# Row spacing of the split weights in a two-layer decoder step, and where the rotary tables lie

## The reference, cut to what matters

```
xp = xp + rmsnorm(mixer(rmsnorm(xp, g_mix_pre)), g_mix_post)      # layer 0: attention + short convolution
xp = xp + rmsnorm(ffn(rmsnorm(xp, g_ffn_pre)), g_ffn_post)        # layer 1: gated spatial MLP as the mixer
def ffn(h, w_up, w_down):
    a = jax.nn.relu(h @ w_up)                                     # 2048 -> 8192
    return (a * a) @ w_down                                       # 8192 -> 2048
def rope(x, pos):                                                 # on queries and keys of layer 0
    return jnp.concatenate([x1 * cos - x2 * sin, x2 * cos + x1 * sin], axis=-1)
```

## Time and profile before

| | us |
|---|---|
| median of 3 runs | 2230.07 |
| lowest and highest of them | 2228.09, 2232.19 |
| the profiled execution | 2228.98 |
| its span, first to last instruction | 2227.3 |
| PE busy in the span | 2176.4 |
| PEld busy | 2154.9 |
| DVE busy | 1249.9 |
| ACT busy | 995.6 |
| POOL busy | 236.9 |

### The profile page before, as it was taken

The page is one execution under the profiler, slowest core; times in us unless marked ns, Lnnn a source line. Parts: engine busy times, 40 slices in busy tenths (PEclk is TensorE's granted clock), DMA queues, the critical chain, the costliest instruction groups (busy, mean ns, idle before and its releaser), DMA issues.

```text
span 2227.3 us, 43497 instructions
## 1 busy us (share of the span) xinstructions
PE 2176.4 (98%) x17771; PEld 2154.9 (97%) x17771; DVE 1249.9 (56%) x1318; ACT 995.6 (45%) x1243; POOL 236.9 (11%) x178
## 2 busy tenths in 40 slices
PE   7999998999999999999989999989999999999999
PEld 7999998999999999999979999979999999999998
DVE  7556756654554455455576675575445545545543
ACT  5545444443443344344454564444334434434443
POOL 3001213000000000011251201220000000001112
PEclk9999998999999999999999999989999999999999
DMA  6854453655655655565535455545555555555551
GB/s 218 232 171 136 155 183 113 189 177 181 187 174 186 215 181 186 176 185 172 186 114 188 155 170 181 178 127 176 188 175 183 183 177 187 174 184 183 176 181 65
DMA packets 380630, 386.72 MB, mean 174 GB/s; under 512 B 6804, under 2 KB 378316, under 8 KB 380430
## 3 DMA queue, kind: packets, MB, share of 16 engines
q1 hardware_dynamic: 374530, 380.02, 54.4%
q10 hardware_dynamic: 6036, 5.80, 0.8%
HBM read 380.10 MB, written 5.71 MB: 173 GB/s over the span
## 4 chain that ended last, share of the span: by engine, by line
PE 92%; DVE 6%; ACT 1%; DMA 0%; issue 0%; DVEq 0%; SPq 0%; ACTq 0%
PE ps L1353 30%; PE ps L1355 30%; PE ps L1354 30%; DVE hlo L979 2%; DVE wlo L952 1%; DVE y L1001 1%; ACT whi L586 0%; PE ps L1635 0%; DMA region<-in_x_prompt_dram 0%; PE ps L1704 0%; PE ps L1548 0%; PE ps L1534 0%; PE ps L1467 0%; DVE region L1336 0%; DVE y L1006 0%; DVE x L1007 0%
## 5 line engine op out<-in xcount | busy, mean ns | idle before, releaser
L952 DVE TENSOR_TENSOR wlo<-raw,whi 128x1024 fp32r<-128x1024 f32 x712 | 895.2, 1261 | 805.0 <-ACT whi L586 804.6
L586 ACT ACTIVATE whi<-raw 128x1024 fp32r<-128x1024 f32 x712 | 752.3, 1059 | 1066.4 <-PE ps L1355 1061.3
L1353 PE MATMUL ps<-hhi,whi 128*128 128x264 f32 x3136 | 902.6, 288 | 33.4 <-DVE hlo L979 33.1
L1354 PE MATMUL ps<-hlo,whi 128*128 128x264 f32 x3136 | 895.4, 286 | 0.0
L1355 PE MATMUL ps<-hhi,wlo 128*128 128x264 f32 x3136 | 895.3, 285 | 0.0
L1353 PE MATMUL ps<-ahi,whi 128*128 128x264 f32 x2560 | 727.0, 284 | 0.0
L1355 PE MATMUL ps<-ahi,wlo 128*128 128x264 f32 x2560 | 726.8, 284 | 0.0
L1354 PE MATMUL ps<-alo,whi 128*128 128x264 f32 x2560 | 726.6, 284 | 0.0
L1353 PEld LDWEIGHTS ps<-hhi,whi 128*128 128x128 f32 x3136 | 595.5, 190 | 43.5 <-issue 30.1
L1355 PEld LDWEIGHTS ps<-hhi,wlo 128*128 128x128 f32 x3136 | 595.4, 190 | 0.0
L1354 PEld LDWEIGHTS ps<-hlo,whi 128*128 128x128 f32 x3136 | 595.1, 190 | 0.1
(11 more groups left out here) (218 smaller groups left out, 763.6 us busy)
## 6 DMA issues: line engine op xcount, KB each, us to landing
raw<-in_w_ffn_up_dram SPq DMA_DIRECT2D x128, 1024.0 KB, 5.3
raw<-in_w_ffn_down_dram SPq DMA_DIRECT2D x128, 1024.0 KB, 5.5
raw<-in_w_in_even_dram SPq DMA_DIRECT2D x36, 1024.0 KB, 5.1
raw<-in_w_in_cmlp_dram SPq DMA_DIRECT2D x32, 1024.0 KB, 5.3
raw<-in_w_out_even_dram SPq DMA_DIRECT2D x16, 1024.0 KB, 5.5
raw<-in_w_out_cmlp_dram SPq DMA_DIRECT2D x16, 1024.0 KB, 5.6
region<-in_x_prompt_dram SPq DMA_DIRECT2D x4, 512.0 KB, 9.1
out_y_prompt_dram<-region SPq DMA_DIRECT2D x8, 256.0 KB
```

Of the source, the lines that this page charges most:

```text
L586: act.activation(whi[:, QK * q:QK * q + QK, :], raw[:, 2 * par + q // 2, k, :], ACT.Copy).then_inc(w_hi_ready, 1)
L952: dve.tensor_tensor(wlo[:, QK * q:QK * q + QK, :], raw[:, 2 * par + q // 2, k, :], whi[:, QK * q:QK * q + QK, :].bitcast(F32), ALU.subtrac ...
L1353: pe.matmul(out, whi[:, k, cols], hi[:, k, ::-1], start=(k == 0), stop=False)
L1354: pe.matmul(out, whi[:, k, cols], lo[:, k, ::-1], start=False, stop=False)
```

## The change

The tiles whi and wlo get rows of 264 words, of which the first 256 are used. A row therefore takes 1056 bytes, as a row of the activations does. This needs 512 bytes more for each of the two tiles. The tiles cos and sin are no longer allocated; their names now stand for rows 14 and 15 of y. The compiled addresses are now: whi 33920, wlo 50816, hhi 101504, hlo 118400, ahi 135296, alo 152192. Every engine has the same instructions in the same order as before, with the same waits; the write of whi and the write of wlo now go to four pieces of 256 words, 264 apart, where they went to 1024 words in one piece. Tiles declared after sin lie 1088 bytes lower than before, those from x to mean_w 1024 bytes higher.

```diff
@@ -52,6 +52,7 @@
 BC = 256
+WROW = T
@@ -93,8 +94,8 @@
         raw = sb("raw", [P, 4, 2 * QK, BC])
-        whi = sb("whi", [P, CH, BC], F32R)
-        wlo = sb("wlo", [P, CH, BC], F32R)
+        whi = sb("whi", [P, CH, WROW], F32R)[:, :, 0:BC]
+        wlo = sb("wlo", [P, CH, WROW], F32R)[:, :, 0:BC]
@@ -104,8 +105,8 @@
-        cos = sb("cos", [P, T])
-        sin = sb("sin", [P, T])
+        cos = y[:, 14, :]
+        sin = y[:, 15, :]
```

## The result

| | before | changed |
|---|---|---|
| median, first comparison | 2230.07 (5 runs) | 2219.06 (5 runs, 2216.87 to 2221.27) |
| median, second comparison (after_again) | 2230.08 (9 runs) | 2218.65 (5 runs, 2217.33 to 2219.21) |
| profiled execution, and its span | 2228.98, 2227.3 | 2220.41, 2218.7 |

The ratio is 0.9951 with an interval of 0.9937 to 0.9966 in the first comparison and 0.9948 (0.9934 to 0.9961) in the second: faster by 11.0 and by 11.4 us. The forecast was 2218.1, with a range of 2212.0 to 2229.5.

A forecast was written before the change was run, and what follows sets the result against it. PE's matmul pace was taken as the bound, slowed where its two reads meet. 172 blocks times 0.07 us gave 12.0 us, other parts nothing: 2228.98 to 2216.98, plus 1.09 for the median, 2218.1; range 2212 to 2229.5.

The forecast's parts named there:

- Reading of the bound: PE's matmul pace sets the time; rows 2, 3 and 4 of eight together take 2.20 us instead of 2.16.
- phases 64 to 128: Distance from weight row to activation row, modulo 256 bytes; at these values PE's two reads were said to meet.
- The slower weight load of the earlier trace: Over k = 2 and 3 PE's weight load is listed with 189 ns instead of 188, cited as showing both streams matter.
- Saving per block: Sixteen clean rows make a block of 11.52 to 11.55 us instead of 11.60: 0.05 to 0.08 us saved, 0.07 taken.
- Number of blocks: 172 blocks gain, without block 0, the first after each of three normalisations and two more around the layer-1 mixer.
- The inner band: Total of 2213 to 2222 us around 2218.1, from savings of 13.9 and 8.3 with 1 us of scatter; chance 0.72.
- Writes in four pieces: Writes of whi and wlo by ACT and DVE: costed at nothing, between -20 and +20 ns a write.
- loads from any multiple of 32 bytes: PE weight loads now start at any multiple of 32 bytes, as the transposes' loads already do: nothing.
- the tables: cos and sin in rows 14 and 15 of y: same shapes, no wait added, nothing.
- the constant phase be a bad one: Rival: the one distance now paid in every row is slow, 11.76 us a block, 2257.6 us in all; chance 0.07.

The follow-up runs named there:

- after_again: The changed kernel unaltered, run again against the kernel before: 2218.65 us, ratio 0.9948.
- before_shift128: The kernel before with a gap of 32 unused words ahead of x, moving the activations under the old weight spacing: 2228.99 us.
- half_load: The changed kernel computing only 64 of 128 columns in the low by high and high by low products (but for row 15 of high by low): 2216.80 us.
- phase32: The changed kernel with a gap of 8 unused words ahead of x, distance 32 bytes modulo 256 in every row: 2219.26 us.
- phase192: The changed kernel with a gap of 48 unused words ahead of x, distance 192 bytes modulo 256 in every row: 2217.13 us.
- tables_alone: The kernel before with only cos and sin moved into rows 14 and 15 of y: 2229.98 us, ratio 1.0001.
- the three bad phases: The changed kernel with gaps of 16, 24 or 32 unused words ahead of x (phases 64, 96, 128): 2265.58, 2248.64 and 2236.80 us.

## Why the prediction was right

**Reading of the bound: right.** PE's pace, and in it the rows at phases 64 to 128, was what could be had. That it is the distance of two rows and not a place was an inference from one unchanging layout; the changed kernel and before_shift128 together show it. Against 0.7208 us for a clean row, rows 1 to 4 of the kernel before lose 0.0009, 0.0175, 0.0134 and 0.0017 us by the trace's nanoseconds: phases 64 and 96 made up 0.031 of the 0.034 us lost in eight rows, and phase 128, which the prediction counted among the slow ones by starts rounded to 0.01, only 0.002. The slower weight load of the earlier trace rows is there too, but slight and at phase 64 alone: 189.1 ns at k = 2, 187.8 to 188.0 in the other rows. It could bear little of the argument. The prediction cited a sentence of the Trainium skill, "TensorE: Matmul & The Clock Gate", Step-by-step, against the change: that loading the next weights takes no read bandwidth from the running matmul. The pace here does depend on the distance of the two: 47 us lie between phases 0 and 64.

**Saving per block: 0.07 forecast, 0.067 measured.** The reason for leaning to 0.07 was wrong in the main. I supposed that the clean rows of before still held a cost of the phase stepping from row to row, which would go. Row 1 held 0.0009 us, which went; rows 0, 5, 6 and 7 took 0.7208 us while the phase stepped, and the rows of the changed kernel take the same 11.53 / 16 = 0.7208. That is 0.0008 above six times 0.120, and in half_load, phase32 and phase192 it is just the same. What that last 0.0008 is, I do not know; 16 of them in 178 blocks are 2 us.

**Number of blocks: 172 forecast, 166 found.** The 11.1 us in both profiles of the changed kernel, block 11 aside, are 166 full savings. The 24 blocks of the layer-1 mixer gave 1.2 us, which is 18 savings; the forecast took off the first of them and two more and so counted 21. So both factors of the 12.0 us were a little high, in the same direction; the two comparisons gave 11.0 and 11.4. The inner band, 2213 to 2222, does not follow from its own terms: 13.9 and 8.3 off 2230.07, with 1 us on either side, are 2215.2 and 2222.8. The normalisations gave nothing, as said: PE waits 33.1 us for hlo in both (the earlier trace rows and the answering row of the changed kernel):

```profile
PE ps L1354 <- DVE hlo L980: 33.1, 20, 8.0
```

**Writes in four pieces, loads from any multiple of 32 bytes, the tables: nothing each.** 1059 and 1261 ns are unchanged to the nanosecond; the floor of 0.120 us with loads that start everywhere shows the second; tables_alone the third, within 2 us.

**The rivals.** That the constant phase be a bad one was rated 0.07 and priced at 2257.6. Its mechanism is real: 2236.8 to 2265.6 at the three bad phases. What kept it away is only that the sizes of the tiles between add up to a multiple of 256 bytes. Its price was read from k = 2 and 3, which the two phases bracket (2265.6 and 2248.6) but do not meet: the pace at a held phase is another one than in passing. My argument against it, that rows at phase 0 took 0.72 in passing, held here, and would have misled for phase 128.
